# Delta rule: the 16x16 diagonal inverses by forward substitution on GpSimd instead of the first four levels of block products

## What is computed

```
L   = strictly_lower(kb @ k.T) * decay
sol = triangular_solve(eye + L, [v * beta, kb * exp(G)])   # u and w
delta = u - w @ S ;  o = (q * exp(G)) @ S + (q @ k.T * decay) @ delta
S   = S * exp(g_last) + (k * exp(g_last - G)).T @ delta
```

## Time and profile before

| | us |
|---|---|
| median of 3 runs | 3852.7 |
| lowest and highest run | 3850.63 and 3857.19 |
| span of the profiled execution, first to last instruction | 3845.6 |
| TensorE busy in it | 3706.3 |
| VectorE, ScalarE, GpSimd busy | 1626.1, 1171.5, 337.2 |

### The profile page before, as it was taken

How to read it: one execution, slowest core, us unless ns; L and a number is a source line. 1 busy time by engine, 2 the same in 40 slices (tenths; PEclk the granted TensorE clock), 3 DMA queues, 4 the chain that set the end, 5 groups by cost and what they waited for, 6 DMA issues and landing times. The chain is left out here.

```text
span 3845.6 us, 53670 instructions
## 1 busy us (share of the span) xinstructions
PE 3706.3 (96%) x20456; PEld 3204.3 (83%) x20456; DVE 1626.1 (42%) x3504; ACT 1171.5 (30%) x2318; POOL 337.2 (9%) x416
## 2 busy tenths in 40 slices
PE   8999999899999999998998999999999999999998
PEld 8999999777777677776667889999999999888886
DVE  4000377655545454544434444444444444432222
ACT  5122222334333333332213333333333333321111
POOL 3000000212111111211200000000000000000000
PEclk9999999899999999999999999999999999999999
DMA  4212322410222212124333331111111111442222
GB/s 156 70 63 65 87 69 70 87 41 24 61 46 46 53 26 48 32 87 144 134 139 105 117 95 46 46 45 45 45 45 45 45 45 48 138 135 82 80 82 67
DMA packets 328015, 278.83 MB, mean 73 GB/s; under 512 B 97106, under 2 KB 292802, under 8 KB 326781
## 3 DMA queue, kind: packets, MB, share of 16 engines
q1 hardware_dynamic: 318207, 258.03, 22.6%
q0 software_dynamic: 5216, 18.23, 1.4%
q10 hardware_dynamic: 4416, 0.14, 0.1%
HBM read 190.70 MB, written 85.65 MB: 72 GB/s over the span
## 5 line engine op out<-in xcount | busy, mean ns | idle before, releaser
L2617 PE MATMUL bank<-ffn_hn_hi,ffn_w_parts 128*128 128x436 f32 (+1 forms) x3520 | 986.4, 361 | 2.2 <-ACTq L2724 2.2
L2617 PEld LDWEIGHTS bank<-ffn_hn_hi,ffn_w_parts 128*128 128x128 f32 x3520 | 661.2, 188 | 38.9 <-issue 2.6
L2617 PE MATMUL bank<-ffn_hn_lo,ffn_w_parts 128*128 128x436 f32 (+1 forms) x1760 | 634.1, 360 | 0.0
L416 PE MATMUL bank<-in_xh,in_wh 128*128 128x436 f32 (+1 forms) x1280 | 357.6, 360 | 2.9 <-DVE in_wh L634 2.9
L2617 PEld LDWEIGHTS bank<-ffn_hn_lo,ffn_w_parts 128*128 128x128 f32 x1760 | 330.8, 188 | 19.3
L2651 PE MATMUL bank<-ffn_down_wa,ffn_g_hi 128*128 (+1 forms) x1224 | 328.9, 391 | 3.9 <-DVE ffn_g_lo L2946 3.9
L2753 ACT COPY ffn_raw<-bank 128x436 f32<-128x436 f32 (+1 forms) x220 | 110.5, 502 | 703.9 <-PE bank L2617 649.4
L1552 PE MATMUL bank<-heads_p_pT,heads_p_v 128*65 128x512 f32 (+3 forms) x640 | 286.4, 529 | 10.3 <-issue 9.8
L2880 DVE TENSOR_SCALAR ffn_hist<-ffn_raw 128x2 f32 (+2 forms) x264 | 45.0, 170 | 546.8 <-ACT ffn_acc L2757 544.0
L2651 PEld LDWEIGHTS bank<-ffn_down_wa,ffn_g_hi 128*128 128x128 f32 x1224 | 230.0, 188 | 53.4 <-DVE ffn_down_wa L2943 3.3
L416 PEld LDWEIGHTS bank<-in_xh,in_wh 128*128 128x128 f32 x1280 | 241.3, 189 | 14.7 <-DVE in_wh L634 3.3
(11 more groups left out here) (418 smaller groups left out, 6369.5 us busy)
## 6 DMA issues: line engine op xcount, KB each, us to landing
ffn_w<-in_w_up_dram SPq DMA_DIRECT2D x44, 512.0 KB, 5.0
ffn_g_raw<-scratch_g SPq DMA_DIRECT2D x110, 192.0 KB, 2.3
scratch_g<-ffn_acc SPq DMA_DIRECT2D x88, 218.0 KB, 2.0
heads_s_k<-in_cache_fox_k_dram SPq DMA_DIRECT2D x8, 2048.0 KB, 13.6
heads_s_v<-in_cache_fox_v_dram SPq DMA_DIRECT2D x8, 2048.0 KB, 8.3
heads_d_qkvT<-scratch_gch SPq DMA_DIRECT2D x17, 768.0 KB, 5.6
ffn_y<-in_w_down_dram SPq DMA_DIRECT2D x22, 512.0 KB, 3.7
scratch_gch<-in_work SPq DMA_DIRECT2D x48, 218.0 KB, 1.9
```

What stands on the lines that cost most here:

```text
L416: mm = pe.matmul(bank[:, 4 + i % 2, 0:wide], a[:, k, :], b[:, k, col:col + wide], start=(k == 0 and m == 0), stop=(k == KD - 1 and m == 2))
L2617: mm = pe.matmul(bank[:, pair(n) + e, 0:width], w_parts[a][:, part, e, k, :], x[:, k, cols], start=(k == 0 and m == 0), stop=(k == KD - 1 ...
```

## The change

Level 0 and the levels 1 to 3 go. In their place, for every chunk:

1. SyncE stores the eight 16x16 diagonal blocks (of four heads) of `LT` to a scratch array in DRAM, with 8 DMAs of 64 pieces of 64 bytes, at planned start + 16.8. It waits for `LT`.
2. SyncE loads the array back with one DMA, one block per partition (32 partitions of 1 KB), at planned start + 19.6.
3. GpSimd solves all 32 blocks at once: one masked product of 256 elements, one memset of the diagonal, and for j = 1 to 14 a product and a subtraction on j x (15 - j) elements; 30 instructions, each of which waits for the one before.
4. SyncE stores the 32 inverses with one DMA, at planned start + 35.6.
5. SyncE loads them into the diagonal blocks of `xd`, a tile that is zero elsewhere, with 8 DMAs of 64 pieces of 64 bytes, at planned start + 38.1.
6. TensorE transposes `xd` at planned start + 40.6, ScalarE copies it to `X`, and the levels 4 to 6 follow from planned start + 42.6 (`level_at`). The streams' chunk has no level and no transpose any more, and uses `xd`.

`solve(t)` takes the place of level 0 in GpSimd's stream, ahead of `output(t - 1)` and `weigh_z(t)`.

```diff
+    FIRST = 4
+    SOLVED = 41.0
...
     def level_at(self, t, n):
-        return self.start(t) + 18.0 + self.ROOTS + (n - 1) * 6.0
+        return self.start(t) + self.SOLVED + self.ROOTS + (n - self.FIRST) * 6.0
...
+    def store_blocks(self, sp, t):
+        s, DS = self.s, self.DS
+        sp.wait_ge(s["lt_ready"], 2 * t + 1)
+        after(sp, s["l_moved"], self.MOVED * t)
+        for b in range(self.NB):
+            at = slice(b * DS, (b + 1) * DS)
+            sp.dma_start(self.io["l_blocks"][b].rearrange("h j i -> j h i"), self.LT[at, :, at]).then_inc(s["l_moved"], 16)
+
+    def load_blocks(self, sp, t):
+        s = self.s
+        sp.wait_ge(s["l_moved"], self.MOVED * t + 16 * self.NB)
+        after(sp, s["x_step"], self.SOLVE * t)
+        sp.dma_start(self.l_blk, self.io["l_blocks"].rearrange("b h j i -> (b h) j i")).then_inc(s["l_moved"], 16)
+
+    def store_inverse(self, sp, t):
+        s = self.s
+        sp.wait_ge(s["x_step"], self.SOLVE * (t + 1))
+        after(sp, s["x_moved"], self.MOVED * t)
+        sp.dma_start(self.io["x_blocks"].rearrange("b h c i -> (b h) c i"), self.x_blk).then_inc(s["x_moved"], 16)
+
+    def load_inverse(self, sp, t):
...
+        sp.wait_ge(s["x_moved"], self.MOVED * t + 16)
...
+        for b in range(self.NB):
+            at = slice(b * DS, (b + 1) * DS)
+            sp.dma_start(self.xd[at, :, at], self.io["x_blocks"][b].rearrange("h c i -> c h i")).then_inc(s["x_moved"], 16)
...
         for t in range(NC + 1):
+            late = self.start(t) + self.ROOTS
+            yield late + 15.2
+            self.store_blocks(sp, t)
+            yield late + 18.0
+            self.load_blocks(sp, t)
             yield self.start(t) + 30.0
             if t >= 1:
                 store(t - 1)
...
                 load_z(t + 1)
+            yield late + 34.0
+            self.store_inverse(sp, t)
+            yield late + 36.5
+            self.load_inverse(sp, t)
...
-            yield late + 17.6
-            pe.wait_ge(s["lt_ready"], 2 * t + 1)
-            pe.wait_ge(s["xt0_ready"], t + 1)
-            for h in range(GH):
-                mm = pe.transpose(self.at(t, 1, h), self.XT[:, h, :], ident)
-            mm.then_inc(s["x0_mm"], 1)
-            for n in range(1, self.levels(t)):
+            if not self.streams(t):
+                yield late + 39.0
+                pe.wait_ge(s["x_moved"], self.MOVED * (t + 1))
+                for h in range(GH):
+                    mm = pe.transpose(self.at(t, 1, h), self.xd[:, h, :], ident)
+                mm.then_inc(s["xt_mm"], 1)
+            for n in range(self.FIRST, self.levels(t)):
...
+        def solve(t):
+            DS, n = self.DS, self.SOLVE * t
+            rest = c["block_rest"][0:c["BLOCKS"], :].rearrange("p (c i) -> p c i", i=DS)
+            pool.wait_ge(s["l_moved"], self.MOVED * (t + 1))
+            after(pool, s["x_moved"], self.MOVED * t)
+            nc.gpsimd.tensor_tensor(self.x_blk, self.l_blk, rest, ALU.mult).then_inc(s["x_step"], 1)
+            pool.wait_ge(s["x_step"], n + 1)
+            diagonal = self.x_blk.rearrange("p c i -> p (c i)")[:, 0:DS * DS:DS + 1]
+            nc.gpsimd.memset(diagonal, 1.0).then_inc(s["x_step"], 1)
+            for j in range(1, DS - 1):
+                pool.wait_ge(s["x_step"], n + 2 * j)
+                shape = [c["BLOCKS"], j, DS - 1 - j]
+                some, x = self.outer[:, 0:j, j + 1:], self.x_blk[:, 0:j, j + 1:]
+                nc.gpsimd.tensor_tensor(some, spread(self.x_blk[:, 0:j, j:j + 1], shape),
+                                        spread(self.l_blk[:, j:j + 1, j + 1:], shape), ALU.mult).then_inc(s["x_step"], 1)
+                pool.wait_ge(s["x_step"], n + 2 * j + 1)
+                nc.gpsimd.tensor_tensor(x, x, some, ALU.subtract).then_inc(s["x_step"], 1)
...
-            pool.wait_ge(s["lt_ready"], 2 * t + 1)
-            nc.gpsimd.tensor_tensor(self.x0[:], self.LT[:], spread(c["level0_t"][:].unsqueeze(1), [P, GH, P]), ALU.mult) \
-                .then_inc(s["pool_x0"], 1)
-            pool.wait_ge(s["pool_x0"], t + 1)
-            nc.gpsimd.tensor_tensor(self.XT[:], self.x0[:], spread(c["ident"][:].unsqueeze(1), [P, GH, P]), ALU.add) \
-                .then_inc(s["xt0_ready"], 1)
+            solve(t)
...
                 output(t - 1)
             weigh_z(t)
```

More of the change, by code:

```diff
@@ L99, in make_constants @@
     keep(c["before_q"][:], [[DS, DB], [1, DS]], 0, -1)
-    for n, m in enumerate(c["level"]):
+    for n, m in c["level"].items():
         s = 1 << n
@@ L107, in make_constants @@
         keep(v[:, :, 0, :], [[2 * s, P // (2 * s)], [0, s]], 2 * s - 1, -1)
[L109 to L113, removed]
+    block = c["block_rest"][0:c["BLOCKS"], :].rearrange("p (c i) -> p c i", i=DS)
+    step(nc.gpsimd.memset(block, -1.0))
+    keep(block, [[-1, DS], [1, DS]], -1, 0)
     step(nc.gpsimd.memset(later[:], 1.0))
@@ L780, in __init__ @@
         self.LEVELS, self.LEVELS_S = 7, 4
-        assert (1 << self.LEVELS) == P and (1 << self.LEVELS_S) == c["DS"]
+        assert (1 << self.LEVELS) == P and (1 << self.LEVELS_S) == c["DS"] and self.FIRST == self.LEVELS_S
+        self.NB, self.DS = P // c["DS"], c["DS"]
+        self.LV, self.SOLVE = self.LEVELS - self.FIRST, 2 * (c["DS"] - 1)
+        self.MOVED = 16 * self.NB + 16
+        assert self.NB * GH == c["BLOCKS"] <= P
         self.banks = banks
@@ L1051, in tensor @@
                 yield l + 3.6
[L1052 to L1053 removed]
+                pe.wait_ge(s["w_ready"], self.LV * t + m + 1)
+                if m == 0:
                     pe.wait_ge(s["lt_ready"], 2 * t + 2)
                 else:
[L1056 to L1058 removed]
+                    pe.wait_ge(s["xt_ready"], (self.LV - 1) * t + m)
+                if n == self.levels(t) - 1:
+                    pairs(t, 2, self.wn, self.XT, "y_mm")
                 else:
[L1060 removed]
+                    pairs(t, 2, self.XT if m else self.xd, self.wn, "y_mm")
             yield self.last_at(t) + 0.8
[L1062 removed]
+            if self.streams(t):
+                pe.wait_ge(s["x_moved"], self.MOVED * (t + 1))
+                pe.wait_ge(s["unitT_out"], 4 * t + 4)
+            else:
+                pe.wait_ge(s["xt_last"], t + 1)
             pe.wait_ge(s["pool_scaled"], 2 * t + 2)
[L1064 removed]
+            pairs(t, 0, self.kbG, self.xd if self.streams(t) else self.XT, "wt_mm")
             yield from (finish_streams(t) if self.streams(t) else finish(t))
@@ L1093, in scalar @@
                 nc.scalar.copy(dst[:], self.heads(t, r)).then_inc(s["unitT_out"], 1)
[L1094 to L1097, removed]
+            if not self.streams(t):
+                yield late + 40.0
+                act.wait_ge(s["xt_mm"], self.LV * t + 1)
+                nc.scalar.copy(self.X[:], self.heads(t, 1)).then_inc(s["x_ready"], 1)
+            for n in range(self.FIRST + 1, self.levels(t)):
                 yield self.level_at(t, n) + 2.6
-                act.wait_ge(s["xt_mm"], (self.LEVELS - 2) * t + n - 1)
+                act.wait_ge(s["xt_mm"], self.LV * t + n - self.FIRST + 1)
                 nc.scalar.copy(self.XT[:], self.heads(t, 0)).then_inc(s["xt_ready"], 1)
@@ L1220, in vector @@
             dve.wait_ge(s["kk_mm"], 2 * t + 1)
+            after(dve, s["l_moved"], self.MOVED * t)
             tt(self.LT[:], self.heads(t, 1), self.dec[:], V).then_inc(s["lt_ready"], 1)
@@ L1224, in vector @@
             tt(self.AT[:], self.heads(t, 2), self.dec[:], V).then_inc(s["lt_ready"], 1)
-            for n in range(1, self.levels(t)):
-                l = self.level_at(t, n)
+            for n in range(self.FIRST, self.levels(t)):
+                l, m = self.level_at(t, n), n - self.FIRST
                 yield l + 2.2
-                dve.wait_ge(s["w_mm"], (self.LEVELS - 1) * t + n)
+                dve.wait_ge(s["w_mm"], self.LV * t + m + 1)
                 tt(self.wn[:], self.heads(t, 1), spread(c["level"][n][:].unsqueeze(1), [P, GH, P]), V) \
@@ L3053, in build @@
         ("mix_tok", (TOK, FH * FD + GH * DV)), ("h_tok", (TOK, D)), ("g", (F2 // 2, TOK)))}
+    for name in ("l_blocks", "x_blocks"):
+        scratch[name] = nc.dram_tensor(f"scratch_{name}", (P // DS, GH, DS, DS), F32, kind="Internal").ap()
     scratch["c_rows"] = nc.dram_tensor("scratch_c_rows", (2, c["FH"], SEQ), F32, kind="Internal").ap()
@@ L3075, in sb @@
                     return constants.enter_context(nc.sbuf_tensor(name, shape, F32))
-                for n in ("ones", "tri", "tri_s", "same_stream", "causal", "after", "decay_mask", "decay_mask_s",
-                          "level0_t"):
+                for n in ("ones", "tri", "tri_s", "same_stream", "causal", "after", "decay_mask", "decay_mask_s"):
                     c[n] = sb(n, [P, P])
-                c["level"] = [sb(f"level{n}", [P, P]) for n in range(7)]
+                c["level"] = {n: sb(f"level{n}", [P, P]) for n in range(Delta.FIRST, 7)}
+                c["block_rest"] = sb("block_rest", [P, DS * DS])
```

44 lines of the change are left out of this document (25 added, 19 removed).

## The result

The kernel with the change takes 4058.2 us (median of 4 runs, 4057.1 to 4061.7) against 3854.9 us for the kernel before on the same chip (4 runs): a ratio of 1.0531, 95% interval 1.0515 to 1.0548, or 203 us slower. The forecast was 4085 us, in a range of 3925 to 4270. In its own profile the span is 4057.1 us. Of all executions in this document one, of the kernel named "The solve without its steps", was far slower (11925.6 us), and its time is the median of the other three.

What follows compares the result with a forecast made beforehand. TensorE was taken to bound the kernel. Per chunk, wait 16.6 plus clock 2.5 less gain 6.7 and absorbed 1.0 gave 11.4, times 16 = 182; with 5 for the streams and 45 for crowded chunks, 3852.7 + 232 = 4085 us, range 3925 to 4270.

Steps and rivals of the forecast that it cites:

- What bounds the kernel: Whole kernel: TensorE sets the pace, busy 3706.3 of 3845.6 us, taking its stream in an order fixed at build.
- The gain: TensorE work removed per chunk, counted by distances between starts: 6.7 us, 114 over 17 chunks; durations would give 8.3.
- The cover: TensorE's other work from LT's start to the transpose of xd: 18 us, where the plan allots 24 planned us.
- The new chain: From LT's start through stores, load back, solve and inverse's moves into xd: 34.6 us, so TensorE waits 16.6 per chunk.
- The cause named: SyncE's queue: the inverse's store issues 6.0 us after the solve, behind output and z waits, and lands late behind 1 MB.
- The clock: TensorE after each wait: about 5 us of work at half clock, 2.5 us lost per chunk, bounds 0 and 4.5.
- absorbed idle time: TensorE, each period: the wait absorbs 1.0 us of the present 4.3 us idle, bounds 0 and 3.
- the 4146 us: Total time if pieces below 512 bytes doubled every such landing, adding 2 x 1.9 us per chunk, 61 in all.
- crowded chunks: Chunks 5, 0 and 14 to 16, with attention head or cache loads near the chain: 45 us extra in all.
- One thing that the profile should show: TensorE's busy time over the whole kernel falls by 100 to 140 us while the span grows.
- The short chain: LT to xd: issues and solve at their floors, chain 27.2 us, wait 9, total 3905 up to 3985; chance 0.16.
- The faster case: At the transpose of xd, a chain below 23.7 us gains; with no wait 114 us, total 3739; chance 0.05.

Runs made afterwards that it cites:

- The solve without its steps: The solve's 28 products and subtractions left out of the kernel with the change, all moves and waits kept: 3909.4 us, ratio 1.0140 to the kernel before.
- the first three experiments: Against the changed kernel: inverse's moves ahead of output's store and next chunk's loads (3884.6 us); only those loads behind them (3987.0); 28 solve instructions left out (3909.4).
- The second experiment: Against the changed kernel, only the three loads for the next chunk go behind the inverse's moves, the previous output's store stays ahead: 3987.0 us, ratio 1.0335.
- The kernel without the chain: All moves and the solve left out of the changed kernel, xd stays zero, levels 4 to 6 stay: 3742.2 us, ratio 0.9701 to the kernel before.
- the kernel with a chain of 24.7: The changed kernel with the inverse's store and load ahead of the previous output's store and the three loads on SyncE: 3884.6 us, ratio 1.0069.
- the one with 20.9: The changed kernel with the inverse's moves first on SyncE and whole tiles moved in four DMAs: 3803.9 us, ratio 0.9871 to the kernel before.
- the version with whole tiles: The changed kernel with the inverse's moves first on SyncE, LT and xd moved whole in four DMAs: 3803.9 us, ratio 0.9871.

## Why the prediction was right

**What bounds the kernel.** Right. TensorE's fixed order decided: the cover of each chunk is the same to 0.25 us in the kernel after and in the first three experiments (chunk 6: 15.1 us in all four), whatever the chain did behind it. The plan's 24 planned us pass in 18.5.

**The gain.** 6.7 us per chunk and 114 in all were predicted; 6.4 and 114 came out with the chain away. That the total fits to the microsecond is partly luck: 102 us lie in the 16 periods, where 107 were predicted, and 12 outside them, where 7 were. The choice of distances between starts over durations made the difference between 114 and 141.

**The cover.** 18 predicted, 18.5 measured on average, from 15.1 to 23.9 by chunk.

**The new chain.** 34.6 us predicted for an ordinary chunk. Measured in chunk 6 against the steps of the prediction: blocks stored at 6.7 from the start of LT (5.8), loaded at 8.4 (7.9), solved at 18.7 (18.9), inverse's store issued at 24.9 (24.9), landed at 29.4 (29.5), in xd at 34.4 (34.6). That it ends within 0.2 us is partly luck: chunk 6 has one slow store issue, which makes up for a solve and landings that were priced too high. Elsewhere a small store or load followed the one before by 0.45 us, as taken, small pieces landed in 1.5 us instead of 1.9, and the solve took 10.3 us where the two plain rows had priced it at 11: 0.20 us for 14 elements and 0.29 for 56, with gaps of 0.08. Over the fourteen chunks other than 0 and 5 the chain is 34.0 us and the wait 16.0, each 0.6 under the prediction.

**The cause named.** SyncE's order, with the wait for `output` and `weigh_z` and the queued bytes, was put at 6.0 + 2.4 us per chunk; 6.2 + 3.3 came out in an ordinary chunk, and undoing it in all chunks brought back 174 us. The second experiment splits it.

**The clock.** Predicted were 2.5 us per chunk for the clock and 1.0 back for absorbed idle time, 1.5 together; 2.1 came out together. The kernel without the chain splits it: 2.2 for the clock and 0.2 back, so the clock was priced about right, and the absorbed idle time was not there. In chunk 6 the windows show some 3.5 us of work at half clock, a loss of 1.8. The rule of the Trainium skill, TensorE: Matmul & The Clock Gate, section on HAM oscillation, that such a loss is paid again at each wait, is borne out here: the granted clock stood at 0.50 at the end of all 16 waits, and the periods' mean clock is 0.82 to 0.90 in all 16 rows of the windows, against 0.96 to 1.00 before. The rule of the Trainium skill, DMA: Bandwidth & Descriptors, section Specifications, on pieces under 512 bytes did not show in the landings: the DMAs of 64 pieces of 64 bytes landed in 1.5 to 1.6 us (medians), sooner than the 1.7 of a 128 KB store, so the 4146 us worked out beside it were too high.

**What was mis-sized.** The change of time was put at 232 us and is 203. From LT to LT the sum had 182 us and most of 45 for crowded chunks, and 198.5 came out; the 45 is the term that failed. The 16 waits sum to 267.9 us, and 16 of the 16.6 predicted for an ordinary chunk would be 265.6, so 2 us of the 45 show there. Another 14 come from other terms (2.2 for the clock and 0.2 absorbed instead of 2.5 and 1.0, a gain of 6.4 instead of 6.7), which brought the forecast nearer to the result by luck. Chunk 5 did cost 10 us extra (wait 26.7 instead of 16.7). But chunk 0 had a longer chain (41.6) under a longer cover (23.9), and its wait of 17.7 is ordinary; and chunks 13 to 15, near the cache loads, waited 18.9, 12.5 and 15.4. I priced what lengthens the chain and not that the cover differs too. One thing that the profile should show came out otherwise: TensorE's busy time was to fall by 100 to 140 us and fell by 62. Busy time counts work at half clock at about twice its length (the four transposes of line 1084 show 1.11 us, the four of level 0 showed 0.63), so it is no measure of work taken away here; the kernel without the chain is, where it fell by 99.

**The rivals.** The short chain needed all floors at once, and few held: the landing of small pieces did, the issues (0.45 us apart, not 0.33), the solve (10.3, not 8.6) and SyncE's queue did not. The faster case's point of decision fits: 23.7 us of chain was said, and with the cover unchanged the kernel with a chain of 24.7 lost 0.7% while the one with 20.9 gained 1.3%.

## What to carry to other kernels

When work goes from a full engine to a chain of DMAs and a slower engine, read two numbers from the timeline before anything else: what the full engine still has to do between the event that starts the chain and the instruction that waits for it, and how long the chain is, with each issue, landing and dependent step. Where a kernel is ordered by planned times, planned distance is no cover; only the work that stands in between is. And put the DMA that somebody waits for ahead of the ones nobody waits for: on one queue in order, the store of an old result and the loads for the next chunk held the new one for 6 us by their waits and issues and another 3 by their bytes. A shorter wait does not make the clock's loss smaller by itself: with the waits cut from 16.7 to 6.1 us on average it was the same, and it shrank in the version with whole tiles, where they are 2.3.

## What was not expected of the hardware

The small DMAs of these kernels cost by their issue more than by their bytes. Eight of 4 KB kept SyncE's queue busy for 3.6 us, as loads and as stores (4.8 to 5.0 us in the four chunks with one slow issue of a store, and 9.7 once, for the loads of chunk 0, behind those of an attention head), and each landed in 1.5 to 1.6 us; one of 256 KB was issued in 0.36 us and landed in 2.3. GpSimd's small instructions kept to one line over a range of sizes, 0.20 us at 14 elements, 0.29 at 56 and 0.72 at 256, so a chain of 30 could be priced from a one-element row and a 512-element row within 0.7 us.
